# Retention decays loaded once, and the entry of a two-block transformer kernel reordered

## The chip, the cores and the metric

The kernel runs on one core of a Trainium2 chip. The metric is device time in microseconds (us), the median of three runs. One program launch computes both blocks below from inputs in HBM to an output in HBM.

## What is computed

Two transformer blocks follow each other on 512 tokens of width 1024. All of it is float32. Only the parts around the change are shown.

```python
def first_block(x, p, attn_norm_g, w_in, b_f, ...):
    h = rms_norm(x, attn_norm_g)
    proj = h @ w_in                       # q, k, v, f_logit, cb, cc, cu, ga, gb
    q, k = per-head rms_norm of q and k
    log_f = log_sigmoid(f_logit + b_f)    # 8 heads; its cumulative sum c biases the logits
    y_att = forgetting_attention(q, k, v, log_f)
    y_conv = cb * causal_short_conv(cc * cu, conv_w)
    merged = sigmoid(ga) * (y_att @ w_out_att) + sigmoid(gb) * (y_conv @ w_out_conv)
    x = x + merged @ w_o
    ...                                   # mixture of experts, per-layer embedding

def second_block(x, c, ctx, c_ctx, w_mod, ..., a_f, a_b, ...):
    mod = silu(c) @ w_mod + b_mod         # and the same for c_ctx
    h = modulate(rms_norm_2(x, norm1_w), sh1, sc1)
    q, k, v, g, f = split_proj(h @ w_in)  # k, v of the context too, for the first state
    # retention in both directions; decay of head h: gamma = exp(-exp(a[h]))
    o = bidir_retention(q, k, v, a_f, a_b, s_f, s_b)
    ...                                   # readout, Fourier branch, gates, convolutional FFN
```

The retention uses tables made of powers of gamma: one of all pairs of positions in a chunk (near), one that scales queries by their position (q_reach), one that scales keys (k_reach), and one factor for a whole chunk (step).

## The kernel before

Activations lie transposed: a tile has 128 features as partitions and 512 tokens as columns, and x is eight such tiles (KC = 8). Every weight passes through one of two slots, j = 0 or 1. SP loads 16 tiles of 128 x 128 into `raw[j]` (`load_slot`). ScalarE copies them to `w_hi[j]` in a rounded format (`split_hi`), DVE subtracts to get `w_lo[j]` (`split_lo`), and TensorE multiplies (`product`: hi by hi, hi by lo, lo by hi, three matmuls for each pair of tiles). Semaphores count slots g through the whole kernel: raw_in, hi_ready, lo_ready, chunk_done. The load of slot g waits for the w_lo of slot g - 2, the split of slot g for the products of slot g - 2. Each engine runs its own program in order, stage by stage. SP issues all loads, in program order; no other engine issues one here besides the indirect ones of POOL.

**Entry.** `start_sync` loads constants (small), four tiles of x by tokens (x_in), slot 0 (G_FORGET, 8 tiles) and slot 1 (G_MIX, 16 tiles), and then 19 small vectors into v_in and bias_f. `start_scalar` squares the x tiles with a sum per token (x_ss), splits slot 0, runs `norm_rstd` (a tiny Ln on `warm` that makes the table load come early, then Ln and Exp of the mean), splits slot 1, and writes h_hi eight times. `start_tensor` turns x (32 transposes), makes the mean over features as a matmul of ones with diagonal matrices x_diag, turns the vectors, and runs four matmuls for nothing (`keep_warm`). `start_vector` copies the turned x from PSUM, writes x_diag after its fourth copy, splits w_lo of slot 0, copies the turned vectors to vec, and then runs `norm_dve`: for each of eight tiles pre (x times gain times rstd) and h_lo (pre minus h_hi). `start_gpsimd` (POOL) splits w_lo of slot 1.

**Forget gate and first pair of heads.** `forget_tensor` multiplies slot 0 (the forget logits) and the first half of slot 1 together, tile by tile, as h_lo becomes ready. `forget_scalar` splits slot 2 when the forget product is done, then computes the log-sigmoid (Identity, Abs, Exp, Ln), then silu of the two conditioning vectors. `forget_vector` ends it with a scan to c_row. In `mix_tensor` the second half of slot 1 follows, then v is turned, c_row is turned (`forget_turn`), and slot 2 begins.

**Retention.** `ret_sync` loads slots G_RET and G_RET + 1, then constants (dist, rope), the decay logits, the store of x to scratch_x (2 MB), and slots G_RET + 2 and on. The eight decays of each direction are loaded in three layouts: `decay` (all heads on all partitions), `decay_row` and `decay_st` (a quarter of the columns, by head parity on halves of the partitions). `ret_scalar` runs the norm, writes h_hi, waits for all of these loads (t_const, 192), takes Exp of the three, and then goes on to `pair`, whose first step is the split of slot G_RET + 1.

Of the kernel before, what the change touches and what calls it, by code (L numbers as in the profile page):

```python
# [167 lines left out]
def build(nc, a, const, out):  # L168
# [7 lines left out]
    with root:  # L176
# [337 lines left out]
        def norm_rstd(act, n, bank=7):  # L514

            act.activation(warm[:, n:n + 1], ones[:, 0:1], ACT.Ln)
# [43 lines left out]
        S = semaphores("x_in0", "x_in1", "v_in", "small_in", "x_turned", "v_copied", "x_sq", "x_diag")  # L560
# [10 lines left out]
        def start_sync(sp):  # L571
# [6 lines left out]

            n = 0
            for name, at, row, rows in VECTORS:  # L580
                sp.dma_start(v_in[row:row + rows, 0, :], a[name].rearrange("(r n) -> r n", n=P))\
                   .then_inc(S["v_in"], 16)
                n += 1
            for row, name in ((V_QG, "q_norm_g"), (V_KG, "k_norm_g")):
                for h in range(2):
                    sp.dma_start(v_in[row:row + 1, 0, 64 * h:64 * h + 64], a[name].rearrange("(r n) -> r n", r=1))\
                       .then_inc(S["v_in"], 16)
                    n += 1
            w2 = a["conv_w_2"].rearrange("(r n) -> r n", n=P)
            sp.dma_start(v_in[:, 1, :], w2[0:P, :]).then_inc(S["v_in"], 16)  # L590
            sp.dma_start(v_in[0:4, 2, :], w2[P:P + 4, :]).then_inc(S["v_in"], 16)
            sp.dma_start(v_in[4:48, 2, :], a["conv_b_2"].rearrange("(r n) -> r n", n=P)).then_inc(S["v_in"], 16)
            sp.dma_start(v_in[48:96, 2, :], a["b_mod_2"].rearrange("(r n) -> r n", n=P)).then_inc(S["v_in"], 16)
            sp.dma_start(bias_f[:, :], a["b_f"].rearrange("(r n) -> r n", n=1)).then_inc(S["v_in"], 16)
            assert 16 * (n + 5) == V_DMAS

        def start_scalar(act):

            for i in range(NT):
# [6 lines left out]
            split_hi(act, G_FORGET, 0, 8)  # L606
            act.wait_ge(G["x_ready"], 1)
            norm_rstd(act, N_ATT, 0)
            split_hi(act, G_MIX, 1)
            norm_hi(act, N_ATT)  # L610

        def start_tensor(pe):
# [9 lines left out]
            pe.wait_ge(S["x_diag"], NT)  # L622
            pe.wait_ge(G["x_ready"], 1)
            for i in range(NT):
                done = pe.matmul(psum[:, 0, i * P:(i + 1) * P], ones[:, :], x_diag[:, i, :], start=True, stop=True)
            done.then_inc(G["ms_ready"], 1)
# [4 lines left out]
            done.then_inc(S["x_turned"], 1)  # L631
            pe.wait_ge(G["x_ready"], 3)
            keep_warm(pe, 2, 4)

        def start_vector(dve):
# [6 lines left out]
            for c in range(KC):  # L642
                dve.wait_ge(S["x_turned"], c + 1)
                dve.tensor_copy(x[:, c, :], psum[:, c, :]).then_inc(G["x_ready"], 1)
                if c == 3:
# [4 lines left out]
            split_lo(dve, 0, 0, 8)  # L650
# [4 lines left out]
            norm_dve(dve, N_ATT, lambda c: vec[:, V_ATT_G + c:V_ATT_G + c + 1])  # L655

        def start_gpsimd(pool):
            pool.wait_ge(G["lo_ready"], 1)
            split_lo(pool, G_MIX, 1)
# [14 lines left out]
        def forget_tensor(pe):  # L674
# [4 lines left out]
            for k in range(KC):  # L679
# [4 lines left out]
                if k == 0:  # L684
                    pe.wait_ge(G["lo_ready"], 2)
# [12 lines left out]
        def forget_scalar(act):  # L698
            split_hi(act, G_MIX + 1, 1 - G_MIX % 2)
# [9 lines left out]
            act.wait_ge(W["wm_mod"], 1)  # L709
            act.wait_ge(W["wm_silu"], 1)  # L710
            act.wait_ge(S["v_copied"], 1)
            for v in range(2):
                act.activation(silu_c[:, :, v:v + 1], vec[:, V_C + 8 * v:V_C + 8 * v + 8]
                               .rearrange("p (k o) -> p k o", o=1), ACT.Silu).then_inc(W["wm_silu"], 1)

        def forget_vector(dve):
# [8 lines left out]
            dve.tensor_tensor_scan(c_row[:, :], f_one, f_z, 0.0, ALU.mult, ALU.add).then_inc(FG["c_row"], 1)  # L725
            dve.wait_ge(FG["c_col"], 1)
# [126 lines left out]
        def mix_tensor(pe):  # L853
# [31 lines left out]
            def pair(m, rest):  # L885
# [14 lines left out]
                if rest[0] is not nothing:  # L900
                    pe.wait_ge(M["m_ga"], 2 * m)
                half_slot(pe, j, 1, of_halves, 1)
# [5 lines left out]
                done.then_inc(M["m_v_turned"], 1)  # L908
# [2190 lines left out]
```

## Time and profile before

| what | value |
|---|---|
| median of 3 runs | 1641.6 us (1640.71 to 1642.41) |
| profiled execution | 1644.22 us |
| span of its trace | 1642.5 us |
| TensorE busy | 1577.3 us, 96% |
| VectorE (DVE) busy | 902.4 us, 55% |
| ScalarE (ACT) busy | 775.5 us, 47% |
| GpSimd (POOL) busy | 121.2 us, 7% |
| mean granted TensorE clock | 0.982 of full |

The profile shows one execution. Times are microseconds from the start of the span. PE is TensorE's matmuls, PEld its weight loads, DVE is VectorE, ACT ScalarE, POOL GpSimd, SPq the DMA issues of SyncE. L436 is line 436 of the kernel. Matmuls are pipelined, so a busy PE is not PE at its peak. The share of a chain or of busy time is an average over stages; what a change in one stage is worth is read from the wait that ends last there. "idle before <- releaser" gives the idle time of an engine ahead of an instruction and what ended it.

### The profile page before, as it was taken

What the parts mean: (1) busy time and instruction counts of PE and PEld (TensorE: products, weight loads), DVE (VectorE), ACT (ScalarE), POOL (GpSimd) and SP (SyncE); (2) the same over time, 40 slices, a digit from 0 to 9 for tenths busy, and PEclk for the clock granted to TensorE, in tenths of its full rate; (3) what the DMA queues carried; (4) which work ended last, traced back from release to release, by engine and by line L of the source; (5) the groups of instructions that cost most, each with busy time, mean ns of one, the idle gap of its engine ahead of it and who ended that gap; (6) DMA issues with size and microseconds to landing.
All of it is one profiled execution on the core that took longest, in us unless ns stands there. A gap on an engine that the chain in (4) does not pass through costs nothing.

```text
span 1642.5 us, 19995 instructions
## 1 busy us (share of the span) xinstructions
PE 1577.3 (96%) x7623; PEld 1266.5 (77%) x7623; DVE 902.4 (55%) x1114; ACT 775.5 (47%) x923; POOL 121.2 (7%) x94
## 2 busy tenths in 40 slices
PE   6999999999999899989799999999999999999998
PEld 4776777788777678878588888887887788888886
DVE  5434343444578778977452553544365565555564
ACT  4645445322557678856443343354124443343334
POOL 1101011000023233310010000000000000000000
PEclk8999999999989999999899999999999999999999
DMA  5446564224089999942321212231432323333221
GB/s 150 142 167 215 182 220 150 74 80 141 34 300 356 341 339 352 335 155 77 121 77 52 77 51 76 66 98 53 154 99 56 96 85 102 101 96 103 83 84 71
DMA packets 182033, 230.43 MB, mean 140 GB/s; under 512 B 14906, under 2 KB 153462, under 8 KB 178639
## 3 DMA queue, kind: packets, MB, share of 16 engines
q1 hardware_dynamic: 174367, 217.13, 40.1%
q0 software_dynamic: 7600, 12.41, 2.1%
q8 instruction: 43, 0.70, 0.2%
q14 instruction: 23, 0.19, 0.0%
HBM read 226.52 MB, written 18.37 MB: 149 GB/s over the span
## 4 chain that ended last, share of the span: by engine, by line
PE 83%; DMA 6%; DVE 4%; ACT 3%; issue 2%; SPq 1%; POOL 0%; POOLq 0%; DVEq 0%; ACTq 0%
PE psum L459 21%; PE psum L460 20%; PE psum L461 20%; DMA hg<-h_rows,at_row 2%; DMA y_rows<-y_sb,at_row 2%; PE psum L759 1%; PE psum L1865 1%; PE psum L1867 1%; PE psum L1866 1%; PE psum L841 1%; DMA vec<-in_ret_decay_b 1%; DVE pre L538 1%; PE psum L1246 1%; PE psum L1248 1%; PE psum L1247 1%
## 5 line engine op out<-in xcount | busy, mean ns | idle before, releaser
L459 PE MATMUL psum<-h_hi,w_hi 128*128 128x512 f32 x1160 | 463.3, 399 | 7.7 <-DVE w_lo L436 3.3
L460 PE MATMUL psum<-h_lo,w_hi 128*128 128x512 f32 x1160 | 454.1, 391 | 0.0
L461 PE MATMUL psum<-h_hi,w_lo 128*128 128x512 f32 x1160 | 454.1, 391 | 0.0
L436 DVE TENSOR_TENSOR w_lo<-raw,w_hi 128x2048 fp32r<-128x2048 f32 (+2 forms) x99 | 223.6, 2259 | 236.7 <-ACT w_hi L432 236.7
L459 PEld LDWEIGHTS psum<-h_hi,w_hi 128*128 128x128 f32 x1160 | 219.0, 189 | 67.9 <-issue 16.7
L461 PEld LDWEIGHTS psum<-h_hi,w_lo 128*128 128x128 f32 x1160 | 218.9, 189 | 47.1
L460 PEld LDWEIGHTS psum<-h_lo,w_hi 128*128 128x128 f32 x1160 | 219.3, 189 | 44.4 <-issue 1.4
L432 ACT ACTIVATE w_hi<-raw 128x2048 fp32r<-128x2048 f32 (+2 forms) x100 | 187.9, 1879 | 75.7 <-PE psum L461 67.4
L489 ACT ACTIVATE sq<-x 128x512 f32<-128x512 f32 x56 | 35.3, 631 | 146.3 <-DVE x L1359 84.1
L1813 DVE TENSOR_TENSOR w_lo_more<-raw_more,w_hi_more 128x2048 fp32r<-128x2048 f32 x34 | 77.8, 2287 | 20.2 <-ACT w_hi_more L1806 18.9
L1813 DVE TENSOR_TENSOR w_lo<-raw,w_hi 128x2048 fp32r<-128x2048 f32 x34 | 77.7, 2286 | 15.7 <-ACT w_hi L1806 13.0
L2987 ACT ACTIVATE cv<-psum,vec 128x512 f32<-128x512 f32 x44 | 32.0, 777 | 84.4 <-PE psum L461 84.4
L1806 ACT ACTIVATE w_hi_more<-raw_more 128x2048 fp32r<-128x2048 f32 x34 | 65.0, 1911 | 12.3 <-DMA raw_more<-in_w_up 8.5
L459 PE MATMUL psum<-d_hi,w_hi 128*128 128x512 f32 x176 | 69.3, 394 | 0.0
L460 PE MATMUL psum<-d_lo,w_hi 128*128 128x512 f32 x176 | 69.3, 394 | 0.0
L461 PE MATMUL psum<-d_hi,w_lo 128*128 128x512 f32 x176 | 69.3, 394 | 0.0
L1806 ACT ACTIVATE w_hi<-raw 128x2048 fp32r<-128x2048 f32 x34 | 64.9, 1910 | 2.7 <-DMA raw<-in_w_up 1.9
L3013 DVE SCALAR_TENSOR_TENSOR cv<-psum,vec,cv 128x511 f32<-128x511 f32 x44 | 32.8, 745 | 54.8 <-ACT cv L2987 54.8
L1756 POOL DMA_INDIRECT hg<-h_rows,at_row x22 | 48.0, 2182 | 41.3 <-DVE in_slot L1654 34.7
L459 PE MATMUL psum<-hc_hi,w_hi 128*128 128x256 f32 x96 | 31.2, 325 | 10.8 <-DVE w_lo L436 10.0
L1761 POOL DMA_INDIRECT y_rows<-y_sb,at_row x23 | 29.7, 1293 | 148.0 <-ACT y_sb L1943 140.2
L1359 DVE SCALAR_TENSOR_TENSOR x<-psum,mod,x 128x512 f32<-128x512 f32 x24 | 17.5, 750 | 41.7 <-PE psum L461 41.7
(421 smaller groups left out, 2588.3 us busy)
## 6 DMA issues: line engine op xcount, KB each, us to landing
raw<-in_w_up SPq DMA_DIRECT2D x67, 512.0 KB
wm_raw<-in_w_mod SPq DMA_DIRECT2D x24, 1024.0 KB, 5.1
raw<-in_w_in SPq DMA_DIRECT2D x18, 1024.0 KB
raw<-in_w_in SPq DMA_DIRECT2D x33, 512.0 KB
raw_more<-in_w_down SPq DMA_DIRECT2D x24, 512.0 KB
raw<-in_w_gate SPq DMA_DIRECT2D x23, 512.0 KB
raw_more<-in_w_gate SPq DMA_DIRECT2D x22, 512.0 KB
raw_more<-in_w_up SPq DMA_DIRECT2D x22, 512.0 KB
```

The source lines that it names most:

```text
L432: act.activation(w_hi[j][:, 0:tiles, :], raw[j][:, 0:tiles, :], ACT.Copy).then_inc(G["hi_ready"], 1)
L436: dve.tensor_tensor(w_lo[j][:, 0:tiles, :], raw[j][:, 0:tiles, :], w_hi[j][:, 0:tiles, :].bitcast(F32), ALU.subtract).then_inc(G["lo_ready ...
L459: pe.matmul(to, w_hi[j][:, tile, :], hi_k, start=(k == 0), stop=False)
L460: pe.matmul(to, w_hi[j][:, tile, :], lo_k, start=False, stop=False)
L461: return pe.matmul(to, w_lo[j][:, tile, :], hi_k, start=False, stop=last)
L489: act.activation(sq[:, c % 2, :], x[:, c, :], ACT.Square).then_inc(G["sq_ready"], 1)
L1756: pool.indirect_dma_start(hg[s % 2][:, :], None, h_rows, bass.IndirectOffsetOnAxis(ap=at_row[:, 0, s:s + 1], axis=0), bounds_check=T - 1, ...
L1761: pool.indirect_dma_start(y_rows, bass.IndirectOffsetOnAxis(ap=at_row[:, 1, s:s + 1], axis=0), y_sb[:, :], None, bounds_check=PAIRS - 1, o ...
L1806: act.activation(u_hi[b][:, :, :], raw_of(u)[:, :, :], ACT.Copy).then_inc(E["e_whi"], 1)
L1813: eng.tensor_tensor(u_lo[b][:, :, :], raw_of(u)[:, :, :], u_hi[b][:, :, :].bitcast(F32), ALU.subtract)\
L2987: act.activation(cv[:, s % 2, half, :], psum[:, 2 * ((j0 + s) % 2) + half, :], ACT.Identity, bias=vec[:, bass.ds(V_CONVB + col, 1)], scale ...
L3013: dve.scalar_tensor_tensor(out=buf[:, 1:T], in0=bank[:, 0:T - 1], scalar=vec[:, bass.ds(V_CONV2 + col, 1)], in1=buf[:, 1:T], op0=ALU.mult, ...
```

## The change

It touches three places.

1. Retention: `decay` alone is loaded (two DMAs), exponentiated, and copied on ScalarE into `decay_row` and `decay_st` (four small copies on 64 partitions each). Eight DMAs go. The waits on t_const go from 192 to 64.
2. Entry: ScalarE's queue issues the 19 vector loads, ahead of everything else it does. A tiny Ln comes ahead of the Squares, and `norm_rstd` has none. Slot 1's split is cut in halves: ScalarE splits tiles 0 to 7 before the norm, and tiles 8 to 15 between h_hi of tiles 1 and 2; POOL makes w_lo of slot 0 and then of tiles 0 to 7; DVE makes w_lo of tiles 8 to 15 after `norm_dve`. TensorE turns the vectors before it makes the mean, and DVE writes x_diag after its second copy.
3. Forget gate: both Silus run before the split of slot 2. c_row is turned after the first half of slot 2, and copied after v_tok. TensorE waits for w_lo of slot 1 before that slot's second half.

```diff
-        def norm_rstd(act, n, bank=7):
-            act.activation(warm[:, n:n + 1], ones[:, 0:1], ACT.Ln)
+        def norm_rstd(act, n, bank=7, load=True):
+            if load:
+                act.activation(warm[:, n:n + 1], ones[:, 0:1], ACT.Ln)
...
+        def vectors_in(act):
             n = 0
             for name, at, row, rows in VECTORS:
-                sp.dma_start(v_in[row:row + rows, 0, :], a[name].rearrange("(r n) -> r n", n=P))\
+                act.dma_start(v_in[row:row + rows, 0, :], a[name].rearrange("(r n) -> r n", n=P))\
                    .then_inc(S["v_in"], 16)
...
         def start_scalar(act):
+            vectors_in(act)
+            act.wait_ge(W["wm_free"], 2)
+            act.activation(warm[:, N_ATT:N_ATT + 1], ones[:, 0:1], ACT.Ln)
             for i in range(NT):
...
             split_hi(act, G_FORGET, 0, 8)
+            act.wait_ge(raw_in[1], 32)
+            act.activation(w_hi[1][:, 0:8, :], raw[1][:, 0:8, :], ACT.Copy).then_inc(S["v_split"], 1)
             act.wait_ge(G["x_ready"], 1)
-            norm_rstd(act, N_ATT, 0)
-            split_hi(act, G_MIX, 1)
-            norm_hi(act, N_ATT)
+            norm_rstd(act, N_ATT, 0, False)
+
+            def second_half(c):
+                if c == 1:
+                    act.activation(w_hi[1][:, 8:16, :], raw[1][:, 8:16, :], ACT.Copy).then_inc(G["hi_ready"], 1)
+            norm_hi(act, N_ATT, between=second_half)
...
         def start_tensor(pe):
-            pe.wait_ge(S["x_diag"], NT)
-            pe.wait_ge(G["x_ready"], 1)
-            for i in range(NT):
-                done = pe.matmul(psum[:, 0, i * P:(i + 1) * P], ones[:, :], x_diag[:, i, :], start=True, stop=True)
-            done.then_inc(G["ms_ready"], 1)
             pe.wait_ge(S["v_in"], V_DMAS)
             pe.wait_ge(G["x_ready"], 2)
             for b, rows in enumerate(V_ROWS):
                 done = pe.transpose(psum[:, 1, b * P:b * P + rows], v_in[0:rows, b, :], ident[0:rows, 0:rows])
             done.then_inc(S["x_turned"], 1)
+            pe.wait_ge(S["x_diag"], NT)
+            for i in range(NT):
+                done = pe.matmul(psum[:, 0, i * P:(i + 1) * P], ones[:, :], x_diag[:, i, :], start=True, stop=True)
+            done.then_inc(G["ms_ready"], 1)
...
         def start_vector(dve):
-                if c == 3:
+                if c == 1:
                     dve.wait_ge(S["x_sq"], NT)
...
-            split_lo(dve, 0, 0, 8)
...
             norm_dve(dve, N_ATT, lambda c: vec[:, V_ATT_G + c:V_ATT_G + c + 1])
+            dve.wait_ge(S["v_split"], 2)
+            dve.wait_ge(G["hi_ready"], G_MIX + 1)
+            dve.tensor_tensor(w_lo[1][:, 8:16, :], raw[1][:, 8:16, :], w_hi[1][:, 8:16, :].bitcast(F32), ALU.subtract)\
+               .then_inc(G["lo_ready"], 1)

         def start_gpsimd(pool):
-            pool.wait_ge(G["lo_ready"], 1)
-            split_lo(pool, G_MIX, 1)
+            split_lo(pool, G_FORGET, 0, 8)
+            pool.wait_ge(S["v_split"], 1)
+            pool.tensor_tensor(w_lo[1][:, 0:8, :], raw[1][:, 0:8, :], w_hi[1][:, 0:8, :].bitcast(F32), ALU.subtract)\
+                .then_inc(S["v_split"], 1)
...
         def forget_scalar(act):
+            act.wait_ge(W["wm_mod"], 1)
+            act.wait_ge(W["wm_silu"], 1)
+            act.wait_ge(S["v_copied"], 1)
+            for v in range(2):
+                act.activation(silu_c[:, :, v:v + 1], ..., ACT.Silu).then_inc(W["wm_silu"], 1)
             split_hi(act, G_MIX + 1, 1 - G_MIX % 2)
...
         def mix_tensor(pe):
+                if rest[0] is nothing:
+                    pe.wait_ge(G["lo_ready"], g + 1)
                 half_slot(pe, j, 1, of_halves, 1)
...
-                if rest[0] is nothing:
-                    forget_turn(pe)
                 pe.wait_ge(G["lo_ready"], g + 2)
                 half_slot(pe, 1 - j, 0, of_halves, 0)
+                if rest[0] is nothing:
+                    forget_turn(pe)
...
         def ret_sync(sp):
                             sp.dma_start(decay[:, d, :], a[name].rearrange("(o h) -> o h", o=1)
                                          .to_broadcast([P, RET_HEADS])).then_inc(H["t_const"], 16)
-                            with nc.allow_non_contiguous_dma(reason="every other one of eight numbers"):
-                                for h in range(2):
-                                    sp.dma_start(decay_row[64 * h:64 * h + 64, d, :],
-                                                 a[name].rearrange("(o m h) -> o h m", o=1, h=2)[:, h, :]
-                                                 .to_broadcast([64, 4])).then_inc(H["t_const"], 16)
-                                    sp.dma_start(decay_st[64 * d:64 * d + 64, h, :],
-                                                 a[name].rearrange("(o m h) -> o h m", o=1, h=2)[:, h, :]
-                                                 .to_broadcast([64, 4])).then_inc(H["t_const"], 16)
...
         def ret_scalar(act):
-            act.wait_ge(H["t_const"], 192)
+            act.wait_ge(H["t_const"], 64)
             act.activation(decay[:, :, :], decay[:, :, :], ACT.Exp).then_inc(H["t_dec"], 1)
-            act.activation(decay_row[:, :, :], decay_row[:, :, :], ACT.Exp)
-            act.activation(decay_st, decay_st, ACT.Exp).then_inc(H["t_dec"], 1)
+            act.wait_ge(H["t_dec"], 1)
+            of_head = decay[:, :, :].rearrange("p d (m h) -> p d h m", h=2)
+            for i in range(2):
+                r = slice(64 * i, 64 * i + 64)
+                act.activation(decay_row[r, :, :], of_head[r, :, i, :], ACT.Copy)
+                done = act.activation(decay_st[r, :, :], of_head[r, i, :, :], ACT.Copy)
+            done.then_inc(H["t_dec"], 1)
```

## Rows read from the trace of the kernel before

**Rows 1.** The page: busy time, share of the span, instructions of TensorE.
```profile
PE 1577.3 (96%) x7623; PEld 1266.5 (77%) x7623; DVE 902.4 (55%) x1114; ACT 775.5 (47%) x923; POOL 121.2 (7%) x94
```

**Rows 2.** TensorE's waits, whole span: releaser, us in total, times, longest.
```profile
PE psum L459 <- DVE w_lo L436: 13.3, 3, 10.0
...
PE psum L907 <- ACT v_raw L1019: 1.9, 1, 1.9
```

**Rows 3.** Timeline 0 to 30 us: start, us, engine, instruction, [idle before <- releaser].
```profile
7.88 1.06 ACT L604 ACTIVATE sq<-x_in 128x1024 f32<-128x1024 f32 x1 [5.79 <-DMA x_in<-in_x]
...
8.00 5.31 PE L618 MATMUL psum<-small,x_in 128*128 128x128 f32 x32 [8.00 <-DMA x_in<-in_x]
...
11.81 2.48 DVE L644 COPY x<-psum 128x512 f32<-128x512 f32 x4 [10.39 <-PE psum L618]
...
12.63 1.04 ACT L432 ACTIVATE w_hi<-raw 128x1024 fp32r<-128x1024 f32 x1
...
13.69 1.28 ACT L516 ACT_TABLE_LOAD   x1
...
15.13 1.16 PE L625 MATMUL psum<-x_diag,ones 128*128 128x128 f32 x8 [1.83 <-DVE x_diag L648]
...
18.33 0.63 ACT L521 ACTIVATE rstd<-rstd 128x512 f32<-128x512 f32 x1
...
20.04 0.26 DVE L652 COPY vec<-psum 128x94 f32<-128x94 f32 x1 [1.44 <-PE psum L630]
...
20.63 5.66 DVE L538 SCALAR_TENSOR_TENSOR pre<-x,vec,rstd 128x512 f32<-128x512 f32 x2
20.91 4.83 POOL L436 TENSOR_TENSOR w_lo<-raw,w_hi 128x2048 fp32r<-128x2048 f32 x1 [20.39 <-ACT w_hi L432]
...
26.21 0.68 DVE L545 TENSOR_TENSOR h_lo<-pre,h_hi 128x512 fp32r<-128x512 f32 x1
...
27.04 0.47 PE L459 MATMUL psum<-h_hi,w_hi 128*128 128x512 f32 x1 [1.89 <-DVE h_lo L545]
```

**Rows 4.** The same timeline, DMA issues of SP.
```profile
3.16 7.14 SPq L426 DMA_DIRECT2D raw<-in_w_in  x3
...
10.35 1.63 SPq L581 DMA_DIRECT2D v_in<-in_attn_norm_g  x1
...
12.39 0.29 SPq L581 DMA_DIRECT2D v_in<-in_ffn_norm_g  x1
```

**Rows 5.** Timeline 75 to 78.6 us, DVE beside POOL.
```profile
76.84 1.47 POOL L1196 TENSOR_TENSOR bias_qk<-c_col,c_two 128x768 f32<-128x768 f32 x1 [5.20 <-DVE prob L1074]
...
77.39 0.68 DVE L1166 TENSOR_TENSOR pre<-pre,psum 128x512 f32<-128x512 f32 x1
```

**Rows 6.** Timeline 39 to 48 us, ScalarE.
```profile
39.23 1.92 ACT L432 ACTIVATE w_hi<-raw 128x2048 fp32r<-128x2048 f32 x1 [3.94 <-PE psum L461]
...
46.51 0.58 ACT L1019 ACTIVATE v_raw<-psum 128x512 f32<-128x512 f32 x1
```

**Rows 7.** Stretches: length, busy us by engine, PEclk, DMA share, GB/s.
```profile
49.00:52.20 3.20, 3.20 (x9) 2.47 (x8) 2.80 (x2) 0.89 (x2) 0.00 (x0) 0.50 0.81 196
806.80:820.10 13.30, 5.58 (x25) 5.58 (x26) 3.19 (x6) 5.36 (x8) 0.00 (x0) 0.50 0.85 316
```

**Rows 8.** The chain that ended last, 785 to 815 us: start, us, what.
```profile
791.85 18.06 DMA vec<-in_ret_decay_b
```

**Rows 9.** Timeline around the retention's first split, ScalarE and TensorE.
```profile
800.78 0.73 ACT L530 ACTIVATE h_hi<-pre,mod 128x512 fp32r<-128x512 f32 x1 [0.73 <-DVE pre L538]
809.93 0.22 ACT L2360 ACTIVATE decay<-decay 128x16 f32<-128x16 f32 x1 [8.43 <-DMA vec<-in_ret_decay_b]
...
810.25 1.89 ACT L432 ACTIVATE w_hi<-raw 128x2048 fp32r<-128x2048 f32 x1
...
814.52 0.58 PE L459 MATMUL psum<-hc_hi,w_hi 128*128 128x256 f32 x1 [10.05 <-DVE w_lo L436]
```

**Rows 10.** DMA issues: out<-in, queue, KB each, us from issue to landing.
```profile
decay<-in_ret_decay_f SPq DMA_DIRECT2D x1, 4.0 KB, 4.5
```

More of the change, by code:

```diff
@@ L557, in norm_dve @@
                 norm_lo(dve, n, c, shift)
-        S = semaphores("x_in0", "x_in1", "v_in", "small_in", "x_turned", "v_copied", "x_sq", "x_diag")
+        S = semaphores("v_split", "x_in0", "x_in1", "v_in", "small_in", "x_turned", "v_copied", "x_sq", "x_diag")
         VECTORS = (
@@ L585, in start_sync @@
                 for h in range(2):
-                    sp.dma_start(v_in[row:row + 1, 0, 64 * h:64 * h + 64], a[name].rearrange("(r n) -> r n", r=1))\
+                    act.dma_start(v_in[row:row + 1, 0, 64 * h:64 * h + 64], a[name].rearrange("(r n) -> r n", r=1))\
                        .then_inc(S["v_in"], 16)
@@ L589, in start_sync @@
             w2 = a["conv_w_2"].rearrange("(r n) -> r n", n=P)
[L590 to L594, printed above, removed]
+            act.dma_start(v_in[:, 1, :], w2[0:P, :]).then_inc(S["v_in"], 16)
+            act.dma_start(v_in[0:4, 2, :], w2[P:P + 4, :]).then_inc(S["v_in"], 16)
+            act.dma_start(v_in[4:48, 2, :], a["conv_b_2"].rearrange("(r n) -> r n", n=P)).then_inc(S["v_in"], 16)
+            act.dma_start(v_in[48:96, 2, :], a["b_mod_2"].rearrange("(r n) -> r n", n=P)).then_inc(S["v_in"], 16)
+            act.dma_start(bias_f[:, :], a["b_f"].rearrange("(r n) -> r n", n=1)).then_inc(S["v_in"], 16)
             assert 16 * (n + 5) == V_DMAS
         def start_scalar(act):
+            vectors_in(act)
+            act.wait_ge(W["wm_free"], 2)
+            act.activation(warm[:, N_ATT:N_ATT + 1], ones[:, 0:1], ACT.Ln)
             for i in range(NT):
@@ L684, in forget_tensor @@
                 if k == 0:
-                    pe.wait_ge(G["lo_ready"], 2)
+                    pe.wait_ge(S["v_split"], 2)
                 done = product(pe, psum[:, 0, :], 1, of_halves(0, k), h_hi, h_lo, k, k == KC - 1)
@@ L698, in forget_scalar @@
         def forget_scalar(act):
+            act.wait_ge(W["wm_mod"], 1)
+            act.wait_ge(W["wm_silu"], 1)
+            act.wait_ge(S["v_copied"], 1)
+            for v in range(2):
+                act.activation(silu_c[:, :, v:v + 1], vec[:, V_C + 8 * v:V_C + 8 * v + 8]
+                               .rearrange("p (k o) -> p k o", o=1), ACT.Silu).then_inc(W["wm_silu"], 1)
             split_hi(act, G_MIX + 1, 1 - G_MIX % 2)
@@ L708, in forget_scalar @@
             act.activation(f_abs, f_abs, ACT.Ln, bias=1.0).then_inc(FG["f_bias"], 1)
[L709 to L714, printed above, removed]
         def forget_vector(dve):
@@ L725, in forget_vector, with forget_columns @@
             dve.tensor_tensor_scan(c_row[:, :], f_one, f_z, 0.0, ALU.mult, ALU.add).then_inc(FG["c_row"], 1)
+        def forget_columns(dve):
             dve.wait_ge(FG["c_col"], 1)
@@ L908, in pair @@
                 done.then_inc(M["m_v_turned"], 1)
+                pe.wait_ge(G["lo_ready"], g + 2)
+                half_slot(pe, 1 - j, 0, of_halves, 0)
                 if rest[0] is nothing:
                     forget_turn(pe)
-                pe.wait_ge(G["lo_ready"], g + 2)
-                half_slot(pe, 1 - j, 0, of_halves, 0)
                 rest[3]()
@@ L1142, in pair @@
                    .then_inc(M["m_v_tok"], 1)
+                if rest[0] is nothing:
+                    forget_columns(dve)
                 rest[3]()
@@ L2537, in pair @@
                 if rest[0] is nothing:
-                    dve.wait_ge(H["t_const"], 192)
+                    dve.wait_ge(H["t_const"], 64)
                 dve.tensor_copy(kr_t[:, T:T + CTX], kr_raw[:, T:T + CTX])
```

## The prediction, made before the changed kernel was built

> **What bounds the kernel now.** I read the busy shares first, then what TensorE waited for, then the timeline around each wait that the change touches. TensorE has instructions under way for 96% of the span [rows 1], so an edit pays only where it shortens one of its few gaps or a stretch at the lower clock. Its list of waits [rows 2] names two that this change can reach: 10.0 us for one w_lo split, and 1.9 us for v_raw. The rest of the edit lies in the first 27 us, before the first product. The profiled execution took 1644.22 us (span 1642.5), 2.6 above the median 1641.6. I work out differences in it and take them from the median.
>
> **Part 1, the decays (retention stage).** SP issues twelve loads of constants and decays, then the 2 MB store scratch_x and the load of the next weights. The last decay load, from its issue at 791.85, ends 18.06 us later in the chain [rows 8]; by its access pattern it has 256 pieces of four bytes, as seven others have. ScalarE's last h_hi ends at 800.78 + 0.73 = 801.51, then it idles 8.43 us for the decays, and the weight split for slot G_RET + 1 stands behind that wait in its queue. That split starts at 810.25, DVE's follows, and TensorE starts at 814.52 [rows 9]. The change drops the eight loads in small pieces. The first decay load landed in 4.5 us [rows 10]; the second now follows it directly and should be in by about 792, ten us before ScalarE asks. So this wait goes entirely, and ScalarE's own end of h_hi is late next. Three tiny activations took 0.32 us from 809.93 to 810.25 [rows 9]; now there are five and a wait, about 0.6 us, so the split starts near 802.15, not 810.25: **8.1 us earlier**. The store and the load behind it are issued about 5 us earlier and no longer queue behind the small pieces; I cost them at nothing, since ScalarE needs that next weight slot only at 806. If they were still slow, ScalarE's next split would wait, but it has some 10 us before TensorE wants it.
>
> TensorE would then idle 1.9 us here, not 10.0. Through the stretch 806.8 to 820.1 the granted clock was 0.50 [rows 7], that is 1.2 GHz, with TensorE at work for 5.58 us of it. After the 1.9 us gap for v_raw [rows 2] there were 3.2 us at 0.50 [rows 7]. In 5.58 us at half speed 2.8 us are lost, in 3.2 us 1.6, so 1.2 come back; the matmuls here are half as wide, and I take **1.0 us**. The bounds are 0 and 2.8 (no slow stretch). Part 1: 9.1 us.
>
> **Part 2, the entry.** Step by step, from the timeline [rows 3] and SP's issues [rows 4].
> - ScalarE issues the 19 vector loads. No row shows an issue on ScalarE. SP's small ones took 0.29 us each, its first 1.63 (a queue still full), and its three big weight issues 7.14 together [rows 4]. I take 0.3 (the nearest in kind): 0.8 + 5.7 = 6.5. The bounds are 0.29 and 1.63 each. They go to the same DMA engines as the x tiles, through a queue that was empty.
> - The table load and the tiny Ln now come before the Squares: 1.28 + 0.2 (from the load at 13.69 to 15.19) gives 8.0, and the first Square stood at 7.88. The x tiles set this anyway. The vectors' 163 KB beside them may cost up to 0.5 us; I take 0.2, so the squares end near 13.0 (12.7 before).
> - DVE copies two tiles (2.48 / 4 = 0.62 each from 11.81), ending at 13.05. x_diag takes it to about 14.0 (four operations on a quarter of a tile's columns; x_diag and the mean's start lay inside 14.3 to 15.13 before), six more copies to 17.7. It no longer splits w_lo here; POOL does. The vector copies (20.04 to 20.63, 0.6) take it to 18.3; before, they waited for SP's last vector.
> - TensorE turns the vectors after the x tiles (13.3 to about 14.0) and makes the mean at 14.05 to 15.2. It is done 1.1 us earlier than before (15.13 + 1.16 = 16.29). From there to the end of Exp were 2.67 us (18.96), so rstd is ready at 17.9. ScalarE meanwhile splits two halves (1.04 each, 13.0 to 15.1) just in time.
> - POOL's one 4.83 us split, from 20.91 to 25.74, is the real cost of this stage: two pre operations, of some 0.7 us each, took 5.66, and h_lo started only at 26.21. In the change it does two of half that length: 14.1 to 16.5, and 16.5 to 18.9. Does it hold up DVE's copies from PSUM? The nearest rows say no: DVE's L1166, with one PSUM operand, took 0.68 inside a POOL operation of 1.47 [rows 5]. The first pre, with x and rstd in SBUF, would be ready at 18.3 and held until 18.9, and ends near 19.5.
> - pre, h_hi and h_lo then follow in 0.65 us steps: h_lo starts at 20.15. The first product came 0.83 us after that before, so now at about 21.0, not 27.04: **6.0 us**. The second half of slot 1 is split on DVE behind the eight h_lo (about 1.4 us for each pre and h_lo: to 31.3, then a quarter of POOL's time, 1.2: 32.5). TensorE needs it about 12.2 us after its first product (39.23 - 27.04, [rows 3, 6]), at 33.2: 0, with 0.7 us of cover. The extra 1.04 us on ScalarE between h_hi(1) and h_hi(2) fits partly into its gaps; even all of it would cost TensorE only 0.3.
> - Keep-warm matmuls, released by the third copy (14.6), end before 21, so a gap of up to 3 us stands ahead of the first product instead of the 1.89 of now [rows 3]. I keep the present loss to a slow clock behind it: 0; the bounds are 1.6 either way.
>
> **Part 3, ScalarE between the forget product and v_raw.** From the split at 39.23 to v_raw at 46.51 it ran the split, four small activations, two table loads (1.28 each, as at 13.69) and both Silus [rows 3, 6]. The Silus and their load move ahead of the split, into its idle 3.94 us. But Exp then finds the Silu table and needs its own load: 1.28 out, 1.28 in, and only the Silus (about 0.25) are saved. They end about when the split may start, so up to 0.2 of that could be lost: I take **0.2 us**. The scan for c_row comes 1.3 us later against v_raw, but its turn moved behind half a slot (about 5.5 us of products), and the bias it feeds is used only with the first scores, more than 15 us on. The load of slot G_MIX + 2 now waits for DVE's half split (32.5 rather than 25.7, when POOL ended), needed behind v_raw at 41: nothing.
>
> The Trainium skill, page "ScalarE: Activation LUTs", section "What ACT_TABLE_LOAD costs", gives 2.66 us a switch with its drain. Here the load at 13.69 began 0.02 us after the split before it (12.63 + 1.04) and took 1.28 [rows 3]. By the page's figure the Squares would start 1.4 us later and the result would be an estimated 1.4 us slower than my sum; the rows decide.
>
> **Sum.** 9.1 + 6.0 + 0.2 = 15.3; less 0.2 for the x tiles' later arrival on TensorE: 15.1. Profiled execution 1644.2 - 15.1 = 1629.1; median 1641.6 - 15.1 = **1626.5**.
>
> **The rivals.**
> - *ScalarE's issues stand behind SP's big ones* (0.17). SP's weight issues ran until 10.31 [rows 4]. If ten of ScalarE's 19 wait for those, they end at 13.5, the Squares start at 15.0, seven us late, and DVE stands at x_diag with six copies behind it. The pre work starts near 24.8, the first product at 27.2: the entry gives nothing. 1641.6 - 9.1 = 1632.5. For it: 1.63 us on SP's next small issue. Against it: that is SP's own queue.
> - *POOL holds DVE's copies after all* (0.07). 4.8 us of POOL falls among 3.7 us of copies; the copies end near 22, and the first product comes near 24.6: 1630.1.
> - *Part 1 gives nothing* (0.05): the remaining loads land late, or the split waits for something else behind them. 1641.6 - 6.0 = 1635.6.
> - *No slow stretch after the shorter gaps* (0.08): one or both of 1.6 us go: 1624.9 to 1623.3. For it: both gaps stay near the 1.9 us that [rows 2, 7] show as enough, and no row shows how much less is. Against it: those same rows.
> - *Slower* (0.03): every ScalarE issue costs the 1.63 us of SP's first [rows 4]. 19 of them end at 31.8, the Squares start 25.3 us late, which turns the entry's 6.2 into a loss of 19; with part 1, +10: 1651.5. It decides from about 1.1 us an issue.
>
> **How the numbers follow.** The forecast has 0.60. A measurement of this kernel tells 0.2% (3.3 us) from no change. Only the last case is slower; all others gain at least 6: faster 0.96, same 0.01, slower 0.03. The range reaches from both slow stretches gone, less 0.8 for the small terms (1622.5), to the first rival plus 1.0 (1633.5); that leaves out part 1 giving nothing and the slower case, and takes in all between.
>
> **What would show it.** Right: ScalarE's wait for decays gone, w_hi at about 802, TensorE's gap there 2 us; DMA at work right after the decays; Squares from 8 to 13; first product near 21; a POOL split ending near 19 and no pre longer than 1.5 us; an Exp load ahead of L706's Exp. Wrong: Squares starting after 10; a long copy or x_diag under POOL; TensorE waiting for the second half's w_lo.

## The result, and the profile after

The changed kernel took 1627.63 us (median, 1624.09 to 1628.87), the one before, measured beside it, 1641.15 (1640.33 to 1642.41). The ratio is 0.9916, with a 95% interval of 0.9903 to 0.9928: 13.5 us less, where 15.1 were forecast (a median of 1626.5). Two later series of the same kernel gave 0.9915 and 0.9906. The profiled execution took 1628.87 us, its span 1627.1 us, 15.4 less than the span before.

The page, and TensorE's waits in the kernel after (releaser, us in total, times, longest), against [rows 1, 2]:

```profile
PE 1573.1 (97%) x7623; PEld 1262.8 (78%) x7623; DVE 897.9 (55%) x1114; ACT 773.6 (48%) x925; POOL 120.6 (7%) x95
```

```profile
PE psum L459 <- DVE w_lo L436: 5.3, 3, 2.6
PE psum L459 <- DVE h_lo L546: 3.2, 1, 3.2
...
PE psum L925 <- ACT v_raw L1037: 1.5, 1, 1.5
```

The 10.0 us wait is gone from the list; in its place stands one of 2.09. The wait ahead of the first product grew from 1.89 [rows 3] to 3.2.

**The retention.** Timeline of the kernel after, 780 to 801 us (start, us, engine, instruction), against [rows 8, 9]:

```profile
780.98 0.43 SPq L2205 DMA_DIRECT2D scratch_x<-x  x1
...
794.79 0.72 ACT L531 ACTIVATE h_hi<-pre,mod 128x512 fp32r<-128x512 f32 x1 [0.73 <-DVE pre L539]
...
795.42 0.20 ACT L2372 ACTIVATE decay<-decay 128x16 f32<-128x16 f32 x1
...
796.30 1.92 ACT L432 ACTIVATE w_hi<-raw 128x2048 fp32r<-128x2048 f32 x1
...
799.34 1.92 ACT L432 ACTIVATE w_hi<-raw 128x2048 fp32r<-128x2048 f32 x1
...
800.60 0.38 PE L459 MATMUL psum<-hc_hi,w_hi 128*128 128x256 f32 x1 [2.09 <-DVE w_lo L436]
```

ScalarE goes from h_hi through Exp and the four copies to the split with no idle time. h_hi comes 5.99 us earlier than before, TensorE 13.92: the stage itself brought 7.93. The next split (799.34) finds its weights loaded.

**The entry.** Timeline of the kernel after, 0 to 22 us, against [rows 3, 4]:

```profile
0.82 0.61 ACTq L583 DMA_DIRECT2D v_in<-in_attn_norm_g  x1
...
1.46 0.31 ACTq L583 DMA_DIRECT2D v_in<-in_conv_w  x1
...
7.94 0.34 ACTq L596 DMA_DIRECT2D bias_f<-in_b_f  x1
8.31 1.28 ACT L603 ACT_TABLE_LOAD   x1 [8.31 <-issue]
...
9.72 1.04 ACT L609 ACTIVATE sq<-x_in 128x1024 f32<-128x1024 f32 x1
...
14.00 0.87 DVE L657 TENSOR_SCALAR x_diag<-small,x_ss 128x128 f32<-128x128 f32 x4 [1.38 <-ACT pre L609]
14.79 3.67 DVE L653 COPY x<-psum 128x512 f32<-128x512 f32 x6
14.93 1.16 PE L639 MATMUL psum<-x_diag,ones 128*128 128x128 f32 x8 [1.70 <-DVE x_diag L657]
14.99 2.36 POOL L436 TENSOR_TENSOR w_lo<-raw,w_hi 128x1024 fp32r<-128x1024 f32 x1 [14.47 <-ACT w_hi L432]
15.87 1.06 ACT L613 ACTIVATE w_hi<-raw 128x1024 fp32r<-128x1024 f32 x1 [0.95 <-DMA raw<-in_w_in]
15.92 2.75 PE L507 MATMUL psum<-small,ones 128*128 128x384 f32 x8
16.83 0.67 ACT L519 ACTIVATE rstd<-psum,eps 128x512 f32<-128x512 f32 x1
17.31 2.35 POOL L672 TENSOR_TENSOR w_lo<-raw,w_hi 128x1024 fp32r<-128x1024 f32 x1
...
19.56 1.41 DVE L539 SCALAR_TENSOR_TENSOR pre<-x,vec,rstd 128x512 f32<-128x512 f32 x2 [0.64 <-ACT rstd L522]
...
21.85 0.76 PE L459 MATMUL psum<-h_hi,w_hi 128*128 128x512 f32 x1 [3.18 <-DVE h_lo L546]
```

The shape is the forecast one. Most steps are some 0.6 to 1 us late (rstd 1.5: ready at 19.44, not 17.9). Neither POOL half stretches pre, as the whole slot did before (5.66 for two, now 1.41). The copies ran at 0.61 each beside both halves.

**The clock.** Stretches of the kernel after (length, busy us by engine, PEclk = granted clock, DMA share, GB/s). The first and third stretch stood at 0.72 and 0.74 in the kernel before; the work of the second ran there from 307.70 to 310.00, at 1.00:

```profile
21.20:28.00 6.80, 6.15 (x15) 4.88 (x16) 6.62 (x11) 3.84 (x6) 0.00 (x0) 0.52 0.18 43
301.70:304.00 2.30, 2.30 (x6) 1.75 (x6) 2.17 (x1) 0.00 (x0) 0.00 (x0) 0.50 0.00 0
800.00:814.00 14.00, 13.40 (x79) 11.40 (x80) 5.99 (x8) 6.16 (x18) 0.00 (x0) 1.00 0.51 152
```

The granted clock stands at 1.2 GHz for about 6.8 us, from the last 0.9 us of the 3.18 us gap on, so TensorE works at it for about 5.9 us. The whole of the second slow stretch goes from about 300.9 to 304.1. None of the retention is slow any more.

### The profile page after: what moved, and what is told of

It reads as the page before. It is cut to its first block, busy times and chain, and to the rows that moved or that the text cites. A ratio compares the mean times of both kernels' runs of the same rounds, so it can differ in the third digit from the quotient of the medians.

```text
span 1627.1 us, 19990 instructions
## 1 busy us (share of the span) xinstructions
PE 1573.1 (97%) x7623; PEld 1262.8 (78%) x7623; DVE 897.9 (55%) x1114; ACT 773.6 (48%) x925; POOL 120.6 (7%) x95
## 4 chain that ended last, share of the span: by engine, by line
PE 87%; DVE 4%; DMA 4%; ACT 3%; issue 2%; SPq 0%; POOL 0%; DVEq 0%; ACTq 0%; POOLq 0%
PE psum L459 21%; PE psum L460 21%; PE psum L461 21%; PE psum L1885 2%; PE psum L1887 2%; PE psum L1886 2%; DMA hg<-h_rows,at_row 2%; PE psum L775 1%; PE psum L857 1%; PE psum L1912 1%; PE psum L1861 1%; DVE pre L539 1%; PE psum L1914 1%; PE psum L1913 1%; PE psum L1266 1%
## 5 line engine op out<-in xcount | busy, mean ns | idle before, releaser
L436 DVE TENSOR_TENSOR w_lo<-raw,w_hi 128x2048 fp32r<-128x2048 f32 (+1 forms) x98 | 222.4, 2269 | 233.9 <-ACT w_hi L432 233.9
L1115 DVE TENSOR_TENSOR d_lo<-psum,d_hi 128x128 f32 (+1 forms) x16 | 4.7, 291 | 64.4 <-ACT d_hi L991 64.4
```

The source lines that it names most:

```text
L436: dve.tensor_tensor(w_lo[j][:, 0:tiles, :], raw[j][:, 0:tiles, :], w_hi[j][:, 0:tiles, :].bitcast(F32), ALU.subtract).then_inc(G["lo_ready ...
```

## The experiments

The theory: part 1 removes a wait and with it a slow stretch; part 2 brings the first product forward because POOL no longer excludes DVE; the parts are independent. Runs e1 to e4 share one measurement of the kernel before (1642.04), e5 to e8 a second (1641.14), e9 to e11 a third (1640.94). In the diffs, lines are cut to what matters.

**e1: the retention part alone, in the kernel before.**

> The kernel before with the retention part of the change alone. Theory (the wait of ScalarE for the eight loads in small pieces is what TensorE's 10 us gap came from, and its long slow stretch went with it): TensorE's gap there 2.1 us instead of 10.0, so 7.9 us, and 1.0 to 2.7 more from the clock, 9 to 10.5 us under the kernel before. The entry stays as it was, with the first product at 27.0. Rival (part of the gain of the full change at this place comes with the entry part, as through another phase of the clock): 7.9 or less.

Measured: 1631.53, ratio 0.9936 (0.9921 to 0.9951), 10.5 us less. TensorE's waits of this run (the other columns as above):

```profile
PE psum L459 <- DVE w_lo L436: 5.3, 3, 2.6
```

Part 1 is worth what the prediction said (9.1) or somewhat more, and needs nothing from the entry.

**e2: the entry and forget gate alone.**

> The changed kernel with the retention part undone: twelve loads, as before. Theory (the parts add up): 4 to 6 us under the kernel before, first product at 21.9, v turned at 42.7, and the 10 us gap in the retention stage is back. With the first run the two gains sum to the full one, 13.5 us, within 1.5 us. Rival (slow stretches of the clock fall at other places when work moves, so that parts don't add): the sum is off by 2 us or more.

Measured: 1636.05, ratio 0.9963 (0.9949 to 0.9978), 6.0 less. The retention's wait is back:

```profile
PE psum L459 <- DVE w_lo L436: 13.2, 3, 10.0
```

The two parts add to 16.5, the whole gave 13.5. That is 3.0 apart, more than the 1.5 expected and than the rival's 2. But the gap is about as large as the intervals (2.5 each way for each part), so the times don't show that the parts hinder each other. The profiles show the same saving with and without the entry: from the start of ScalarE's last h_hi to TensorE's start on the retention's first split it is 13.74 us in the kernel before and 13.70 in e2, 5.81 in the kernel after and 5.80 in e1. What differs between these profiles is where the clock falls, as the rival has it: e2 has a single slow stretch of some 3.4 us in its entry, the full change one of 6.8.

**e3: the entry with slot 1's split undivided, on POOL behind h_hi.**

```diff
             split_hi(act, G_FORGET, 0, 8)
-            act.wait_ge(raw_in[1], 32)
-            act.activation(w_hi[1][:, 0:8, :], raw[1][:, 0:8, :], ACT.Copy).then_inc(S["v_split"], 1)
             act.wait_ge(G["x_ready"], 1)
             norm_rstd(act, N_ATT, 0, False)
-            def second_half(c): ...
+            split_hi(act, G_MIX, 1)
+            norm_hi(act, N_ATT)
```

> The changed kernel with the halves of slot 1 undone: ScalarE splits the whole slot after rstd, POOL makes w_lo of the whole slot in one operation. Theory (POOL and DVE exclude each other where DVE has two SBUF inputs): the POOL operation of 4.8 us starts near 21.4, one pre or h_lo of DVE takes 4 to 5 us again, the first product comes near 26.5, and the median is 4 to 5 us over the changed kernel. Rival (the long pre has another cause, such as DVE waiting for the vectors): no operation of DVE over 1 us, and under 1.5 us over the changed kernel.

Measured: 1632.99, ratio 0.9947 (0.9934 to 0.9960): some 5 us of the change's gain lost. Timeline of this run, 20 to 26 us:

```profile
20.75 4.50 POOL L436 TENSOR_TENSOR w_lo<-raw,w_hi 128x2048 fp32r<-128x2048 f32 x1 [3.34 <-ACT w_hi L432]
21.22 4.57 DVE L546 TENSOR_TENSOR h_lo<-pre,h_hi 128x512 fp32r<-128x512 f32 x1 [0.79 <-ACT h_hi L529]
...
25.94 0.77 PE L459 MATMUL psum<-h_hi,w_hi 128*128 128x512 f32 x1 [7.22 <-DVE h_lo L546]
```

An h_lo of 0.69 us took 4.57 and ended 0.54 after POOL's split. The rest of the entry's edits brought the first pre forward (19.02), and POOL's one long operation then took nearly all of it back: the first product came at 25.94, 4.1 us later than in the kernel after, and at 299 us those 4.1 are still there. The time, 1632.99, is not below that of the retention part alone in the same series (e1, 1631.53). So without the halves the rest of the entry's edits shows no gain. The Trainium skill, page "SBUF — State Buffer", section "Who interferes with whom", says that a DVE instruction with two SBUF inputs contends with a GpSimd instruction that reads SBUF. The row agrees.

**e6: the nineteen vector loads back in SP's queue.**

```diff
-            vectors_in(act)
             act.wait_ge(W["wm_free"], 2)
...
             load_slot(sp, G_MIX, 1, mix_pieces(0, 0))
+            vectors_in(sp)
```

> The changed kernel with the 19 vector loads back on SP's queue, behind the weights; the new order on TensorE stays. Theory (the move to ScalarE's queue carries the entry: the vectors must be there before the mean is made): Squares start at 7.9, but TensorE turns the vectors only at about 19.2 and makes the mean behind them, rstd near 23.5, first product near 26; median 3 to 5 us over the changed kernel. Rival (the entry's gain is all POOL's order): under 1.5 us over it.

Measured: 1630.08, ratio 0.9926 (0.9911 to 0.9941), against 1627.66 and 0.9915 for the changed kernel beside it (e5): 2.4 more by the medians, with intervals that overlap; 3 to 5 were expected. Timeline of this run, 13 to 27 us:

```profile
13.26 2.96 DVE L657 TENSOR_SCALAR x_diag<-small,x_ss 128x128 f32<-128x128 f32 x4
13.72 2.42 POOL L436 TENSOR_TENSOR w_lo<-raw,w_hi 128x1024 fp32r<-128x1024 f32 x1 [13.20 <-ACT w_hi L432]
...
19.12 0.79 PE L635 MATMUL psum<-small,v_in 94*128 94x94 f32 x3 [4.70 <-DMA bias_f<-in_b_f]
...
26.80 0.47 PE L459 MATMUL psum<-h_hi,w_hi 128*128 128x512 f32 x1 [1.37 <-DVE h_lo L546]
```

The mean now waits for the vectors, which TensorE turns ahead of it, and the first product comes 4.2 us later than in e5 (22.60). By the turn of v 2.7 are left of that (45.07 against 42.34), because here no slow stretch follows the first product. So by these rows moving the loads to ScalarE is worth some 3 to 4 us beside the vectors' turn ahead of the mean; the medians alone don't tell their 2.4 from nothing. What the move is worth with TensorE's old order no run shows. The first row holds a surprise: x_diag, 0.87 us for four in the kernel after, took 2.96 (one of the four 2.38) and ended with POOL's half. In the changed kernel ScalarE's later squares happen to keep x_diag clear of POOL.

**e7: the eight small decay loads issued again, into space that nothing reads, with no one waiting for them ahead of the decays.** SP's program waits for them only at the stage's end.

```diff
+                        for d, name in enumerate(("ret_decay_f_2", "ret_decay_b_2")):
+                            for h in range(2):
+                                sp.dma_start(dead[64 * h:64 * h + 64, 0, d, :], ...[:, h, :].to_broadcast([64, 4]))
+                                sp.dma_start(dead[64 * d:64 * d + 64, 1, h, :], ...[:, h, :].to_broadcast([64, 4]))
                         sp.dma_start(scratch_x, x[:, :, :]
```

> The changed kernel with the eight loads in small pieces issued again, behind the two of decay, to a place that is not read; ScalarE waits for none of them. Theory A (only ScalarE's wait cost time): within 1 us of the changed kernel. Theory B (they also hold up the queue): scratch_x and the next weights stand behind them, those weights land at 808 to 812 instead of 792, ScalarE's split of slot G_RET + 2 waits up to 10 us, the tables and v copies behind it on ScalarE come about 4 us late, and TensorE loses 1 to 4 us. My prediction costed this at nothing, so A.

Measured: 1629.99, ratio 0.9935 (0.9921 to 0.9949), 2.3 over e5. First a stretch of it, then its timeline, 783 to 812 us:

```profile
784.00:798.00 14.00, 11.89 (x59) 9.12 (x58) 10.22 (x16) 7.49 (x14) 0.00 (x0) 1.00 0.06 4
```

```profile
783.48 1.54 SPq L427 DMA_DIRECT2D raw<-in_w_in  x1
...
796.00 0.38 PE L460 MATMUL psum<-hc_hi,w_hi 128*128 128x256 f32 x1 [2.11 <-DVE w_lo L437]
...
808.55 1.91 ACT L433 ACTIVATE w_hi<-raw 128x2048 fp32r<-128x2048 f32 x1 [13.70 <-DMA raw<-in_w_in]
810.37 0.58 ACT L2418 ACTIVATE vr_raw<-psum 128x512 f32<-128x512 f32 x1
810.85 0.38 ACT L2419 ACTIVATE vr_raw<-psum 128x256 f32<-128x256 f32 x1
...
811.28 0.58 PE L460 MATMUL psum<-hc_hi,w_hi 128*128 128x256 f32 x1 [5.10 <-ACT vr_raw L2419]
```

The wait for the decays stays away, but a second one stands in its place. For 14 us the DMA engines are busy for a share of 0.06, about one in sixteen, and move 4 GB/s; the weights issued behind the small pieces at 783.48 are ready only at 808.55. ScalarE sits in front of that split for 13.70 us with the copies of v behind it, and TensorE waits 5.10 us for those. From 796.00 to 811.28 TensorE needed 15.28 us for what took 9.61 in the changed kernel (800.60 to 810.21): 5.7 us lost here. A slow stretch follows the 5.10 us gap:

```profile
811.30:814.70 3.40, 3.40 (x16) 3.40 (x17) 3.37 (x5) 3.40 (x13) 0.00 (x0) 0.50 0.11 31
```

With it the loss is 7.1 us: from TensorE's start on the retention to the first product of the FFN stage it is 452.83 us here (796.00 to 1248.83), 445.70 in the kernel after (800.60 to 1246.30) and 445.78 in e5. So both theories fall short, B with its 1 to 4 us too. The spans of the two profiles differ by only 2.6 (1629.7 against 1627.1), because this one has neither the slow stretch of the entry nor that at 301 us and comes to the retention 4.6 us earlier. The median, too, shows only 2.3; where the other runs of e7 won the rest back is not known, since one execution of each kernel was profiled.

In the kernel before the same weights were late too, but nothing came of it: ScalarE waited 4.37 us for them ahead of that split, while TensorE, late itself by the 10 us gap, met no further wait there.

```profile
817.75 1.91 ACT L432 ACTIVATE w_hi<-raw 128x2048 fp32r<-128x2048 f32 x1 [4.37 <-DMA raw<-in_w_in]
```

**e8: the Silus behind Ln again, as before.**

> The changed kernel with the two Silus back behind the log-sigmoid. Theory (a table load only changes its place): Exp needs no load, Silu does, v_raw starts 0.3 us later against the split of slot 2, TensorE's gap is 1.9 us instead of 1.54; median 0.3 us over the changed kernel, and up to 2 if a slow stretch follows the longer gap, as in the kernel before. Rival (the Exp load of the change costs more than it saves): 0.5 us or more under it.

Measured: 1627.04, ratio 0.9918 (0.9905 to 0.9931): 0.6 us under e5. By its size that is what the rival asked for, but it is far inside the intervals, so there is no difference to explain. TensorE's gap before it turns v was 1.89 against 1.54, which is 0.35 us for the Silus, near the 0.3 expected; no measurement of the whole can see it.

**e4: sixteen idle matmuls instead of eight before the first product.** The number of calls (two matmuls each in the trace) is the only edit.

```diff
-            keep_warm(pe, 2, 4)
+            keep_warm(pe, 2, 8)
```

> The changed kernel with eight keep-warm matmuls at the entry instead of four, which fill the gap of 3.2 us between them (end 18.67) and the first product (21.85); they compute nothing that is used. Theory (the 6.8 us at half clock behind that gap come from the gap): no slow stretch between 18 and 30 us, first product unmoved or 0.3 later, 2.5 to 3.3 us under the changed kernel. Rival (the slow stretch comes from something else, or only shifts to the gap for v_raw near 40): within 1 us of the changed kernel.

Measured: 1623.93, ratio 0.9888 (0.9871 to 0.9905). Run again beside the changed kernel (e10 beside e9):

> The changed kernel once more, for the direct comparison with the two kernels beside it. Expected: 1627 to 1628, as in its first two series (1627.63, 1627.66); a gap of about 3.1 us before the first product and a stretch at half clock behind it.

> The changed kernel with sixteen instead of eight idle matmuls (eight calls instead of four; they compute nothing that is used) before the first product, once more, now beside the changed kernel itself. Theory (the 3.1 us gap costs a slow stretch, and filling it saves that stretch): 1624 again, 3 to 4 below the changed kernel of the same call, with no stretch at 0.50 before 400 us in the profile. Rival (its first result lay low by the spread of runs alone): within 1 us of the changed kernel.

Measured: the changed kernel 1625.95, ratio 0.9906 (0.9892 to 0.9921), with sixteen idle matmuls 1624.42, ratio 0.9897 (0.9882 to 0.9912). The difference is 1.5, less than the 3 to 4 expected and more than the rival's 1. Over all series the means are 1626.98 (14 runs of the changed kernel) and 1624.12 (8 runs): 2.9, with an interval of some 1.6 either way from the spread of the runs. Two stretches of e10:

```profile
21.20:28.00 6.80, 6.29 (x28) 4.98 (x28) 6.62 (x11) 3.81 (x6) 0.00 (x0) 1.00 0.19 46
...
299.00:304.00 5.00, 5.00 (x18) 3.92 (x18) 2.21 (x1) 0.00 (x0) 0.00 (x0) 0.78 0.29 65
```

TensorE meets the first of its two waits near 299 us (L867, shown below for the other kernels) at 296.47 in e4 and 296.45 in e10, at 298.24 in e9. The entry stays at 2.4 GHz in both executions, with a gap of 0.5 us instead of 3.2. The stretch at 301 us was absent in e4 (1.00 from 299 to 304) and present in e10, against the expectation. It doesn't explain why e10 fell short: the spans of e4 and e10 are the same, 1621.4, and their medians 0.5 apart. The changed kernel beside e10 was the faster one, 1625.95 after 1627.63 and 1627.66. At 299 us, e10 leads e9 by 1.8, which is what a slow stretch of some 3.4 us in the entry costs. That the gap brings the stretch is not fully shown: in e7 the gap was 3.09 and no slow stretch followed. Filling the gap is a small gain, and this version is the fastest that was measured.

**e11: twelve idle matmuls in the kernel before.**

> The kernel before with twelve instead of eight idle matmuls ahead of its first product (six calls; they compute nothing that is used); nothing of the change. There the gap is 1.89 us and a stretch of 3.4 us at half clock follows it (28.7 to 32.1), and the idle matmuls themselves run at half clock from 19.8 to 25.2. Theory A (the clock falls behind such a gap because of the gap): the gap shrinks to about 0.6, the stretch from 28.7 goes and 1.6 us with it: 1639.5. The stretch at 49.2, behind the 1.9 us wait for v_raw, stays. Theory B (the clock in the entry depends on what ran well before the gap too): the stretch from 28.7 stays or moves, and the time stays within 0.5 of 1641.3. In neither does the first product start earlier than 27.0.

Measured: 1639.64, ratio 0.9991 (0.9982 to 1.0000). The gap shrank to 0.68 us. Two stretches of this run:

```profile
28.70:32.10 3.40, 3.40 (x16) 2.66 (x15) 3.33 (x6) 1.53 (x3) 0.00 (x0) 1.00 0.65 169
48.00:53.00 5.00, 5.00 (x22) 3.78 (x21) 2.77 (x2) 1.01 (x3) 1.02 (x2) 1.00 0.89 288
```

The stretch behind the gap went, as theory A has it, and the time is within 0.2 of what A gave, but only 1.3 under the kernel before, hardly more than nothing. And the stretch at 49, which A wanted to stay, went too, though its gap, for v_raw, is the same (1.88 us against 1.89). By 302 us that is 3.1 us of lead (the first of the two waits, L851, stands at 301.99 against 305.13), of which the median keeps 1.3, so the single profile flatters this version. A gap of 1.9 us is followed by a slow stretch in some kernels and not in others, and gaps are not the whole cause. What else decides was not settled.

**e5: the changed kernel once more**, beside e6 to e8.

> The changed kernel once more, unedited, so that the others of this set stand beside it, and as a second profile of it. Theory (the clock's slow stretches fall differently from run to run, and the rest is fixed): every gap of TensorE outside the expert stage is within 0.2 us of the first profile, first product 21.7 to 22.4, and what differs is where the granted clock was 0.50. Median 1627 to 1629. Rival (the issues and loads of the entry vary themselves): the first product moves by over 1 us.

Measured: 1627.66, ratio 0.9915 (0.9902 to 0.9928). Its slow stretch in the entry has half the length of the first profile's, for a gap of 3.08 instead of 3.18. The first product came at 22.60, 0.2 past the expected range: ScalarE's 19 issues ended at 9.13 instead of 8.28 (one of them took 1.33), and the first Square started at 10.56. So the issues vary themselves, though by less than the rival's 1 us.

## Why the prediction came true, step by step

**Part 1** was forecast as 8.1 + 1.0. The profiles give 7.93 for the wait. Its mechanism held: no idle ScalarE, split at 796.30, next late the h_hi of ScalarE itself, and a TensorE gap of 2.09 (1.9 forecast). The clock's term was mis-sized. From TensorE's start on the retention to that of the FFN stage (its first product after h_lo stood at 1262.95 before and stands at 1246.30) the lead grows from 13.92 to 16.65, by 2.7. That is the upper bound, 2.8, and its condition: behind the 2.09 us gap there was no slow stretch at all. I had taken the 3.2 us stretch behind v_raw as the model of what remains. "The store and the load behind it ... I cost them at nothing" was right for this change, but the reserve named for it was wrong. I said that a late load would have some 10 us before TensorE wanted it. In e7 the load was late, and the copies of v, queued behind the split on ScalarE, cost TensorE a wait of 5.1 us and 7.1 with the clock. The eight loads had two victims; only the first was in my account, and in the kernel before it hid the second.

**Part 2** was forecast as 6.0 at the first product; it is 27.04 - 21.85 = 5.2. The term that was short is the issues. A DMA issue on ScalarE took 0.27 to 0.76, the first 0.61, and the 19 ended at 8.28 instead of 6.5; with the table load they, not the x tiles, set the first Square (9.72, not 8.0). The squares ended at 13.97 instead of 13.0, so slot 0's split and POOL's first half came 0.9 late, and POOL's second half ended at 19.66 instead of 18.9. That end sets the first product: it follows 2.08 or 2.09 us later in e2, e4, e5 and e7 to e10, and 2.19 later here (2.1 in the forecast). A second term was wrong and cost only 0.1: the first half of slot 1 had not landed, and ScalarE waited 0.95 us for it at 15.87, ahead of Ln in its queue, though the mean was ready at 16.09. I had said that ScalarE splits both halves "just in time" and had no row for that landing. But POOL's second half hid nearly all of it: rstd was ready at 19.44, and DVE started pre at 19.56. In the kernel after, e2 and e5 the issues ended at 8.28, 8.82 and 9.13, and the first product came at 21.85, 22.29 and 22.60. The first Square stood at 10.26 and 10.56 in the last two, past the 10 that I had named as a sign of being wrong. DVE's copies under POOL, the value of POOL's halves and the second half's cover held: DVE's w_lo of tiles 8 to 15 was done at 31.96, against my 32.5. Neither rival of the entry came true in the change itself: ScalarE's issues didn't stand behind SP's, and the copies didn't wait for POOL. In e6 x_diag did, which I had named as a sign of being wrong but given no price: its inputs are in SBUF, unlike the copies'.

**Between first product and the pair's second slot** the slow stretch was twice as long as before: the lead falls from 5.19 to 4.06 (ScalarE's split at 35.17 against 39.23). I had set this to 0 with bounds of 1.6. **Part 3**: the next piece, up to v_raw, took 6.94 instead of 7.28, so 0.3 where I took 0.2. Then the stretch at 49 us is gone and the lead returns: at 299 us it is 6.03, seen here on two waits of TensorE in both kernels, first the one before, then the one after:

```profile
305.13 0.33 PE L851 MATMUL psum<-small,y_tok 128*128 128x128 f32 x1 [0.57 <-DVE y_tok L1089]
306.15 0.50 PE L1246 MATMUL psum<-d_hi,w_hi 128*128 128x512 f32 x1 [0.69 <-DVE d_lo L1097]
```

```profile
299.10 0.33 PE L867 MATMUL psum<-small,y_tok 128*128 128x128 f32 x1 [0.57 <-DVE y_tok L1107]
300.12 0.50 PE L1266 MATMUL psum<-d_hi,w_hi 128*128 128x512 f32 x1 [0.69 <-DVE d_lo L1115]
```

So 6.0 of the forecast 6.0 arrive, by luck, since errors cancel: 0.8 late at the first product and a longer slow stretch, against 0.1 more from the Silus and a slow stretch that vanished, which was in no term of mine. The slow stretch at 301 us then takes some 1.7 back, and the expert stage returns it: before, 591.90 to 595.30 ran at 0.54, after, 585.90 to 589.30 at 1.00. At the retention's last h_hi the lead is 5.99.

**The sum.** In the spans it is 6.0 + 7.9 + 2.7 - 1.25 = 15.4; the last term comes behind the 2.6 us wait for w_lo at the start of the FFN stage, which ends 16.65 us earlier than before (1260.56 against 1277.21) and is followed by a slow stretch twice as long. Of the kernel before, and then of the one after:

```profile
1278.30:1281.50 3.20, 3.20 (x10) 2.53 (x9) 2.52 (x4) 1.10 (x2) 0.00 (x0) 0.56 0.97 274
```

```profile
1260.50:1267.00 6.50, 6.44 (x16) 5.04 (x17) 4.36 (x8) 3.37 (x4) 0.00 (x0) 0.52 0.58 161
```

The forecast was 15.1. The medians give 13.5, because the profiled execution of before lay 3.1 above the median measured beside the changed kernel (2.6 above the 1641.6 that I had) and that of after 1.2 above its own. I assumed the same excess for both. It goes with the clock: the four runs of the changed kernel go from 1624.09 at a mean granted clock of 0.992 to 1628.87 at 0.988. That all of it is clock is not shown.

## What to carry to other kernels

Many loads of four-byte pieces were dear twice here: their own consumer waits, and every transfer behind them in the queue is late, so look for who stands behind the split, the copy or the wait that this second one feeds. Cut a long GpSimd operation that reads SBUF into pieces and put them where VectorE reads PSUM; an operation of VectorE with two inputs in SBUF, or x_diag here, cost as much as what was left of the GpSimd one. Then ask what starts the first piece: here the end of the second one set the first product, and DMA issues on ScalarE delayed both. An edit that shifts a kernel's work moves the stretches at half clock too, worth some 1.6 us each here: count them as a spread of both signs rather than as gains.

## What the runs showed of the hardware that was not expected

- The same two gaps (0.57 and 0.69 us, 1.02 us apart) in the same work were followed by no slow stretch in the kernel before and by one in the kernel after (PEclk 0.50 from 301.70 to 304.00). Eleven further profiles have the same two gaps: in five of them (e2, e3, e5, e9, e10) a slow stretch followed, in six (e1, e4, e6, e7, e8, e11) none. The matmuls ahead of the gap are the same ones in all. The gap of 3.1 to 3.2 us before the first product was followed by a slow stretch in five profiles (after, e2, e5, e8, e9) and by none in e7.
- x_diag, a product of an SBUF tile with a scalar of each partition, waits for POOL as an operation with two SBUF tiles does (2.96 against 0.87 us for four, e6). The Trainium skill, page "SBUF — State Buffer", section "Who interferes with whom", names tensor_scalar among the operations that can take the shared ports. This row agrees.
- An issue on ScalarE is dearer than SP's 0.29 [rows 4]: 0.27 to 0.41 for most, 0.61 for the first, 0.76 for one (1.33 for one in e5). The 19 took 7.5 us from the first to the end of the last, where 5.7 were forecast.
